# The second block's down projection as seven block products, with weight sums made by accumulating DMAs

## The reference

```python
h = _rmsnorm(x, g_ffn)
x = x + (jax.nn.silu(h @ w1) * (h @ w3)) @ w2        # w2: 2816 x 1024
gate = jax.nn.sigmoid(_rmsnorm(x, g_ple) @ w_ple_gate)
x = x + gate * (p_i @ w_ple)
return _rmsnorm(x, g_final)
```

## Time and profile before

| | us |
|---|---|
| median of three runs | 2056.28 (2055.24 to 2057.49) |
| span of the profiled execution (first to last instruction) | 2052.9 |
| what lies around the span, against the median | 3.4 |
| TensorE busy | 1952.2 |
| granted TensorE clock, mean | 0.979 |

### The profile page before, as it was taken

The page is one execution under the profiler, slowest core; times in us unless marked ns, Lnnn a source line. Parts: engine busy times, 40 slices in busy tenths (PEclk is TensorE's granted clock), DMA queues, the critical chain, the costliest instruction groups (busy, mean ns, idle before and its releaser), DMA issues.

```text
span 2052.9 us, 22852 instructions
## 1 busy us (share of the span) xinstructions
PE 1952.2 (95%) x9422; PEld 1211.6 (59%) x9422; DVE 730.4 (36%) x1069; ACT 532.1 (26%) x828; POOL 118.6 (6%) x127
## 2 busy tenths in 40 slices
PE   8999999989899897989899899999999999999998
PEld 6867843333333332323333368878888888888886
DVE  5648331101001010100101067595588443345225
ACT  5236220101000000101000056334444332234125
POOL 3432000000000000000000000141000000000000
PEclk9999999999999999999999999999999999999999
DMA  9420789999999999999999933212114222323331
GB/s 273 144 72 18 297 342 430 427 431 429 431 430 432 432 430 427 432 430 429 431 434 425 423 128 134 82 43 83 62 62 146 101 83 82 119 85 113 109 140 59
DMA packets 42295, 517.33 MB, mean 252 GB/s; under 512 B 5216, under 2 KB 5344, under 8 KB 12656
## 3 DMA queue, kind: packets, MB, share of 16 engines
q1 hardware_dynamic: 39728, 508.39, 60.6%
q0 software_dynamic: 2496, 7.92, 1.8%
HBM read 508.92 MB, written 6.29 MB: 251 GB/s over the span
## 4 chain that ended last, share of the span: by engine, by line
PE 73%; DMA 20%; DVE 5%; ACT 1%; issue 1%; POOL 0%; SPq 0%; ACTq 0%; DVEq 0%
DMA arena<-in_w_gu_dram 19%; PE bank L2517 15%; PE bank L2542 6%; PE bank L964 4%; PE bank L963 4%; PE bank L962 4%; PE bank L601 3%; PE bank L602 3%; PE bank L603 3%; PE bank L2479 2%; PE bank L994 2%; PE bank L993 2%; PE bank L995 2%; PE bank L2143 2%; PE bank L2149 2%; PE bank L2145 2%
## 5 line engine op out<-in xcount | busy, mean ns | idle before, releaser
L2517 PE MATMUL bank<-arena 128*64 128x512 f32 x2048 | 480.3, 625 | 67.8 <-DMA arena<-in_w_gu_dram 63.9
L2517 PEld LDWEIGHTS bank<-arena 128*64 128x64 f32 x2048 | 163.1, 143 | 360.2 <-issue 348.0
L3014 DVE TENSOR_TENSOR arena<-arena,bank 128x256 f32<-128x256 f32 x64 | 27.0, 421 | 639.6 <-ACT arena L3255 639.6
L2542 PE MATMUL bank<-arena 128*64 128x512 f32 x1024 | 232.6, 595 | 0.6 <-ACT arena L3259 0.6
L3255 ACT ACTIVATE arena<-bank 128x256 f32<-128x256 f32 x64 | 24.6, 384 | 537.0 <-PE bank L2517 537.0
L2542 PEld LDWEIGHTS bank<-arena 128*64 128x64 f32 x1024 | 73.7, 137 | 139.2 <-issue 139.2
L962 PE MATMUL bank<-input_rounded,weight_rest 128*128 128x512 f32 x352 | 137.2, 390 | 0.0
L964 PE MATMUL bank<-input_rounded,weight_rounded 128*128 128x512 f32 x352 | 137.0, 389 | 0.0
L963 PE MATMUL bank<-input_rest,weight_rounded 128*128 128x512 f32 x352 | 137.0, 389 | 0.0
L601 PE MATMUL bank<-input_rounded,weight_rest 128*128 128x512 f32 x312 | 125.9, 403 | 1.2 <-DVE weight_rest L1050 1.2
L603 PE MATMUL bank<-input_rounded,unit_rounded 128*128 128x512 f32 x312 | 122.4, 392 | 0.0
(11 more groups left out here) (528 smaller groups left out, 2851.1 us busy)
## 6 DMA issues: line engine op xcount, KB each, us to landing
arena<-in_w_gu_dram SPq DMA_DIRECT2D x47, 4096.0 KB, 28.9
arena<-in_w_d_dram SPq DMA_DIRECT2D x62, 2048.0 KB, 26.5
arena<-in_wpack_dram SPq DMA_DIRECT2D x83, 1024.0 KB, 5.0
arena<-in_w_gu_dram SPq DMA_DIRECT2D x32, 2048.0 KB, 17.4
arena<-in_w_d_dram SPq DMA_DIRECT2D x4, 1024.0 KB, 10.0
arena<-in_w_gu_dram SPq DMA_DIRECT2D x3, 1024.0 KB, 8.3
arena<-in_xT_dram SPq DMA_DIRECT2D x4, 512.0 KB, 7.2
arena<-in_x_dram SPq DMA_DIRECT2D x2, 1024.0 KB, 13.2
```

The costliest lines, as they stand in the source:

```text
L2517: last = mm(ab[64 * x:64 * x + 64, :], xsT[:, k, 64 * x:64 * x + 64], w[x][k], start=k == 0, stop=k == KD - 1)
L2542: last = mm(bank[4 + n][64 * x:64 * x + 64, :], hidT[c % 2][:, P * t + 64 * x:P * t + 64 * x + 64], w[:, x, t, 512 * n:512 * n + 512], sta ...
```

## The change

The hidden activations A (512 tokens by 2816) are cut into four blocks: the first and last 256 tokens by the first and last 11 hidden tiles, A11, A12 (first tokens), A21, A22. The weights `w2` are cut alike into B0 (first 11 tiles, first 512 columns), B1 (first tiles, last columns), B2 (last tiles, first columns), B3. Seven products of 11 hidden tiles, two token tiles and 512 columns take the place of eight:

- p1 = A11·B0, ue = (A21−A22)·(B0+B1), p2 = A12·B2, wb = (A11+A21−A22−A12)·B3, vg = (A11+A21−A22)·(B0+B1+B3), zf = (A11+A21)·(B1+B3), hh = A22·(B0+B1+B2+B3).

They run in this order, each in three chunks d of 4, 4 and 3 hidden tiles, so 7 x 11 x 2 x 3 = 462 matmuls. The sums of A are made on VectorE during the up stage (`token_sums`: one addition of 128x256 a tile for the first 11, three for the others). The results reach `x_res` by 22 additions of 128x512 (`down_sums`) in place of eight. The rounded part of a product's activations lies where an operand of an earlier product was.

The sums of weights are made by transfers that add to what lies there (`accum_op=ALU.add`), issued by GpSimd: `grown[d]` is loaded with B0 by SyncE at the end of the up stage and then has B1, B3 and B2 added, each for the next of ue, vg, hh; the chunks of zf are loaded with B1 into the ring and have B3 added there. That is 12 adding transfers of 1 MB or 0.75 MB. Chunks of p1, p2 and wb come by the ring as before.

VectorE's and ScalarE's loops over the up stage are written out. The last gates take the units of the first 256 tokens first, and turning these tokens stands behind zf's second chunk. `hn`, `pw`, `fsilu` and the gate's inputs lie elsewhere.

```diff
+DOWN = ("p1", "ue", "p2", "wb", "vg", "zf", "hh")
+DOWN_GROWN = ("ue", "vg", "hh")
+ADDED = ("ue", "vg", "zf", "hh")
+DOWN_WEIGHT = {"p1": 0, "p2": 2, "wb": 3, "zf": 1}
+DOWN_KS = (range(0, 4), range(4, 8), range(8, HT))
+N_DOWN = 3 * len(DOWN)
...
-GATE_ORDER = [(0, 0), (1, 0), (2, 0), (3, 0), (0, 1), (1, 1), (2, 1), (3, 1)]
+GATE_ORDER = [(0, 0), (1, 0), (0, 1), (1, 1), (2, 0), (3, 0), (2, 1), (3, 1)]
...
+        part_at = {name: B + BLK * i for i, name in enumerate(("a11", "a12", "u", "w", "v", "z", "a22"))}
+        raw_part = {name: view(at, BLK) for name, at in part_at.items()}
+        part_of = {"p1": "a11", "ue": "u", "p2": "a12", "wb": "w", "vg": "v", "zf": "z", "hh": "a22"}
+        part_lo = {m: [rounded(f"down_rest_{m}_{d}", part_at[name] + TOK * ks[0], TOK * len(ks)) for d, ks in enumerate(DOWN_KS)]
+                   for m, name in part_of.items()}
+        hi_at = {"ue": T0 + 1280, "p2": part_at["a11"], "wb": part_at["u"], "vg": part_at["a12"], "zf": part_at["w"],
+                 "hh": part_at["v"]}
+        part_hi = {m: [rounded(f"down_rounded_{m}_{d}", at + TOK * ks[0], TOK * len(ks)) for d, ks in enumerate(DOWN_KS)]
+                   for m, at in hi_at.items()}
...
+        down_bank = {"p1": (4, 5), "ue": (6, 7), "p2": (2, 3), "wb": (4, 5), "vg": (0, 1), "zf": (2, 3), "hh": (0, 1)}
...
+            def add_weights(to, block, d):
+                pool.dma_start(to, A["wpack"][C_DOWN + 3 * block + d][:, 0:512 * len(DOWN_KS[d])], accum_op=ALU.add)\
+                    .then_inc(S(f"added_in{d}"), 16)
+
+            for d in range(3):
+                pool.wait_ge(S(f"grown_in{d}"), nth(f"grown_in{d}", 16))
+                add_weights(grown[d], 1, d)
+            for d in range(3):
+                pool.wait_ge(S(f"added_in{d}"), nth(f"added_in{d}", 16))
+                pool.wait_ge(S("wlo_made"), NFT + 3 * DOWN.index("ue") + d + 1)
+                add_weights(grown[d], 3, d)
+            for d in range(3):
+                c = C_DOWN + 3 * DOWN.index("zf") + d
+                pool.wait_ge(S(f"added_in{d}"), nth(f"added_in{d}", 32))
+                pool.wait_ge(S(f"chunk_in{c % R}"), LANDED[c])
+                add_weights(down_raw(c), 3, d)
+            for d in range(3):
+                pool.wait_ge(S(f"added_in{d}"), nth(f"added_in{d}", 48))
+                pool.wait_ge(S("wlo_made"), NFT + 3 * DOWN.index("vg") + d + 1)
+                add_weights(grown[d], 2, d)
...
+            for m, name in enumerate(DOWN):
+                for d, ks in enumerate(DOWN_KS):
+                    c = C_DOWN + 3 * m + d
+                    if d == 0:
...
+                    pe.wait_ge(S("alo_made"), rests_upto(m, d))
+                    pe.wait_ge(S("wlo_made"), NFT + 3 * m + d + 1)
                     wh = whi[c % R].rearrange("p (k n) -> p k n", n=512)
                     wl = wlo[c % R].rearrange("p (k n) -> p k n", n=512)
-                    for i in range(NT):
+                    for i in range(2):
+                        b = bank[down_bank[name][i]][:, :]
                         for k in ks:
...
+                            mm(b, down_lo(name, k, i), wh[:, k - 4 * d, :], start=k == 0, stop=False)
+                            mm(b, down_hi(name, k, i), wl[:, k - 4 * d, :], start=False, stop=False)
+                            last = mm(b, down_hi(name, k, i), wh[:, k - 4 * d, :], start=False, stop=k == HT - 1)
+                    last.then_inc(S("down_chunk"), 1)
+                    if name == "zf" and d == 1:
+                        pe.wait_ge(S("down_added"), nth("down_added", 14))
+                        turn_tokens(0, range(KD))
+                    if name == "hh" and d == 1:
+                        pe.wait_ge(S("down_added"), nth("down_added", 18))
+                        pe.wait_ge(S("norm_tv"), 3 * KD)
+                        turn_tokens(1, range(4, KD))
 
```

VectorE's sums of the activations, and SyncE's loads:

```diff
+            def token_sums(f):
+                k = f % HT
+                dve.wait_ge(S("act_made"), f + 3)
+                a11, u = tile_part("a11", k), tile_part("u", k)
+                if f < HT:
+                    own(tt(out=tile_part("z", k), in0=a11, in1=u, op=ALU.add))
+                    return
+                if k == 0:
+                    own.wait()
+                own(tt(out=u, in0=u, in1=tile_part("a22", k), op=ALU.subtract))
+                own.wait()
+                own(tt(out=tile_part("v", k), in0=u, in1=a11, op=ALU.add))
+                own.wait()
+                tt(out=tile_part("w", k), in0=tile_part("v", k), in1=tile_part("a12", k), op=ALU.subtract)\
+                    .then_inc(S("sums_made"), 1)
...
+            def part_rest(m, d):
+                name = DOWN[m]
+                dve.wait_ge(S("ahi_made"), rests_upto(m, d))
+                a = slice(TOK * DOWN_KS[d][0], TOK * (DOWN_KS[d][-1] + 1))
+                tt(out=part_lo[name][d], in0=raw_part[part_of[name]][:, a], in1=part_hi[name][d], op=ALU.subtract)\
+                    .then_inc(S("alo_made"), 1)
+
+            def down_rest(m, d):
+                c = C_DOWN + 3 * m + d
+                n = 512 * len(DOWN_KS[d])
+                dve.wait_ge(S("whi_made"), NFT + 3 * m + d + 1)
+                tt(out=wlo[c % R][:, 0:n], in0=down_raw(c), in1=whi[c % R][:, 0:n], op=ALU.subtract).then_inc(S("wlo_made"), 1)
...
+            for m in range(1, len(DOWN)):
+                if m >= 2:
+                    down_sums(m - 2)
+                for d in range(3):
+                    part_rest(m, d)
+                    down_rest(m, d)
+                    if DOWN[m] == "hh" and d == 0:
+                        for k in range(KD):
+                            gate_lo(dve, 0, k)
+                        half_scales(dve, 0)
```

```diff
+                if not in_ring(c):
+                    name, d = down_at(c)
+                    if name == DOWN_GROWN[0]:
+                        if d == 0:
+                            sp.wait_ge(S("up_filled"), 2 * NFT)
+                        elif d == 2:
+                            sp.wait_ge(S("down_chunk"), 2)
+                        sp.dma_start(grown[d], wpack[C_DOWN + d][:, 0:512 * len(DOWN_KS[d])]).then_inc(S(f"grown_in{d}"), 16)
+                    continue
...
+                if C_DOWN <= c < C_PG:
+                    sp.dma_start(down_raw(c), wpack[from_dram(c)][:, 0:512 * len(DOWN_KS[down_at(c)[1]])])\
+                        .then_inc(S(f"chunk_in{c % R}"), 16)
...
+                if c == C_PG:
+                    sp.wait_ge(S("down_chunk"), 18)
                     sp.dma_start(pw.rearrange("p i d -> p (i d)"), ple_kept).then_inc(S("ple_back"), 16)
+            sp.wait_ge(S("wlo_made"), NFT + N_DOWN)
+            sp.dma_start(grow, A["gfin"].partition_broadcast(P)).then_inc(S("gfin_in"), 16)
             tiles = out.rearrange("a (i p) d -> i p (a d)", p=P)
```

More of the change, by code:

```diff
@@ L68, with down_at, in_ring, from_dram @@
 N_CHUNKS = C_PG + N_PG
-C_FIRST = N_CHUNKS
-C_PLE = N_CHUNKS + 1
+D_PG = C_DOWN + 12
+D_FIRST = D_PG + N_PG
+D_PLE = D_FIRST + 1
+def down_at(c):
+    m, d = divmod(c - C_DOWN, 3)
+    return DOWN[m], d
+def in_ring(c):
+    return not C_DOWN <= c < C_PG or down_at(c)[0] not in DOWN_GROWN
+def from_dram(c):
+    if c < C_DOWN:
+        return c
+    if c >= C_PG:
+        return D_PG + c - C_PG
+    name, d = down_at(c)
+    return C_DOWN + 3 * DOWN_WEIGHT[name] + d
+LANDED = {}
+_count = [0] * R
+for _c in range(N_CHUNKS):
+    if in_ring(_c):
+        _count[_c % R] += 16
+    LANDED[_c] = _count[_c % R]
 NSLOT = 8
@@ L501, in program @@
         bhi = [rounded(f"branch_rounded{i}", B + 14336 + WCH * i, WCH) for i in range(2)]
-        actT = view(B + 4096, NFT, L)
-        alo = [rounded(f"hidden_rest{k}", B + 4096 + 512 * k, L) for k in range(NFT)]
-        pw = view(B + 4096, NT, D)
+        pw = view(B + 4608, NT, D)
         pgate = [view(B + 16384 + 512 * i, 512) for i in range(4)]
@@ new lines, in second_dve @@
+            for f in range(NFT):
+                if f % 2 == 0 and f < NFT - 2:
+                    weight_rests(C_UP + f + 2, f + 3)
+                if f == 18:
+                    first_rest(0)
+                if f == 20:
+                    down_rest(0, 0)
+                    first_rest(1)
+                    first_rest(2)
+                act_tile(f)
+                token_sums(f)
+            first_rest(3)
+            down_rest(0, 1)
+            first_rest(4)
+            down_rest(0, 2)
```

395 lines of the change are left out of this document (243 added, 152 removed).

## The result

The changed kernel takes **2071.78 us** (median of 4 runs, 2067.71 to 2072.27); the kernel before 2055.76 (4 runs, 2053.60 to 2057.49). The ratio is 1.007, 95% interval 1.0058 to 1.0083: slower by 16 us by the medians and by 14 by the ratio, where 5.5 us less were forecast and 2064 was the upper end of the range. The profiled execution took 2071.57 us with a span of 2069.8.

What follows compares the result with a forecast made beforehand. TensorE's matmuls, one behind the other, were taken as the bound. −15.0 + 0.3 + 5.0 + 3.6 + 0.6 = −5.5 us, from 2056.3 to 2050.8 us; range 2041.5 to 2064.

Steps and rivals of the forecast that it cites:

- What bounds the kernel, the gain of 15.0: Down stage: TensorE's matmuls are the path, so 66 fewer at 0.2267 us each save 15.0 us.
- p1's second chunk, 0.3: Start of the down stage: VectorE's weight rest for this chunk comes late, so TensorE waits 0.3 us.
- The weights of ue: Deciding term, ahead of ue's first chunk: 3.3 us late plus 1.7 for the lost clock, 5.0 us.
- X − 4.1: TensorE's wait ahead of ue's first chunk, given an adding transfer of X us; forecast at 3.3 us.
- X: Time of GpSimd's adding 1 MB transfer, issue to landing: taken as 7.4 us, bounds 5.0 and 16.4.
- My test for the step: GpSimd's 1 MB transfers land in about 7.4 us; below 6 or above 9, the main step is wrong.
- my own sign: The frame is wrong if TensorE waits at p2, wb or vg, or the up stage's 247 us grow.
- The weights of the others: Products after ue: vg's additions 35 us ahead, zf 3.6 us with clock, hh's second chunk and the gates 0.6.
- X − 5.5: TensorE's wait ahead of zf's first chunk, given an adding transfer of X us; forecast at 1.9 us.
- Slow additions: Rival at ue and zf: adding transfers eat up the gain at X = 10.2; 2066 at X = 15; chance 0.19.
- As quick as plain loads: Rival: additions take X = 5.0 to 5.5, ue waits little, zf not at all; 2043.4 us, chance 0.25.
- VectorE becomes the bound: Rival: six products each start with a 1 us wait while VectorE catches up; 2057, chance 0.14 including other handovers.

Runs made afterwards that it cites:

- e2_none: Changed kernel without GpSimd's twelve down-stage transfers, sums of weights left out: 2043.2 us.
- e1_plain: Changed kernel with the twelve adding transfers as plain loads of the same bytes, sums of weights left out: 17 to 18 us faster than the changed kernel.
- e5_hold: Changed kernel with vg's additions held until wb's last chunk has landed: 3.3 us faster by the ratios.
- e4_gates: Changed kernel with the gate inputs of the first 256 tokens made behind hh's second chunk instead of its first: same ratio as the changed kernel.
- e8_turns: Kernel with order p1, p2, wb, ue, vg, zf, hh and zf's chunks in own memory, now one adding transfer at a time: some 22 us above the expected 2055.
- e12_vg_hold: Reordered kernel with zf's chunks in own memory, ue's additions held for wb's second chunk, now vg's additions issued ahead of zf's: 2049.3 us.
- e11_ue_adds: Changed kernel in which only ue's three transfers add, the other nine fetching plainly: no time in the text; ue waits 4.99 us.
- e3_order: Changed kernel with products in the order p1, p2, ue, wb, vg, zf, hh, all sums made: 2058.3 us.
- e7_spread: Changed kernel with order p1, p2, wb, ue, vg, zf, hh, and zf's chunks loaded 30 to 45 us ahead into own memory: 2054.5 us.

## Why the prediction was wrong

**What bounds the kernel, the gain of 15.0.** Right: e2_none shows 13.9 of it over stage and gates.

**p1's second chunk, 0.3.** Right; it doesn't show above 0.3.

**The weights of ue, the step that decides.** "X − 4.1" was nearly right and X alone was well bounded. ScalarE's and GpSimd's timelines:

```profile
1888.63 0.90 POOL L716 DMA_DIRECT2D arena<-in_wpack_dram  x1 [464.47 <-DMA arena<-in_wpack_dram]
1891.11 0.85 POOL L716 DMA_DIRECT2D arena<-in_wpack_dram  x1 [1.58 <-DMA arena<-in_wpack_dram]
...
1904.89 1.72 POOL L716 DMA_DIRECT2D arena<-in_wpack_dram  x2 [12.93 <-DMA arena<-in_wpack_dram]
```

```profile
1896.55 1.91 ACT L2030 ACTIVATE weight_rounded<-arena 128x2048 fp32r<-128x2048 f32 x1 [8.18 <-DMA arena<-in_wpack_dram]
...
1904.51 1.92 ACT L2030 ACTIVATE weight_rounded<-arena 128x2048 fp32r<-128x2048 f32 x1 [5.11 <-DMA arena<-in_wpack_dram]
```

The first addition took 7.9 us from issue to ScalarE's start, where my X was 7.4; without adding (e1_plain) the same transfer landed in 5.7. By the halved rate that the Trainium skill states (Collectives: The Full Stack, "The bandwidth ceiling: the fold count and why AG ≠ RS ≠ AR") my estimate had been 7.9, and the trace agrees with it. That it is the second fetch which costs the time, and not something else of the same size, no run here separates. `grown[0]` itself landed 1.5 us later than I had it (8.3 behind the stage's start, not 6.8), as three loads left together. 7.9 − 4.1 + 1.5 = 5.3, measured 5.07. With the clock ue cost about 7, not 5.0.

But the second addition, issued 2.5 us behind the first, took 13.4. **The step that failed is that X is one number**, 7.4 us wherever an addition stands, and that additions cost nobody else anything. The sentence "the second and third additions run behind the first ... and don't come late" took each transfer as if it had the DMA engines to itself. At ue itself that did little harm: TensorE waited 0.21 and 0.55 us ahead of these two chunks. It is at zf, wb and hh that the sharing costs. Here only additions are under way (zf's third and hh's first two), to be held against 426 GB/s at a share of 0.99 in the earlier trace rows:

```profile
1979.00:1982.00 3.00, 3.00 (x15) 2.49 (x14) 2.13 (x2) 0.11 (x1) 0.00 (x0) 1.00 1.03 205
```

All engines full at 205 GB/s: a megabyte (1.05 million bytes) holds them for 5.1 us, where a plain one holds them for 2.5. Twelve transfers of 11 MB together are some 56 us of full engines. My test for the step was a landing outside 6 to 9 us: it was 12.7. By my own sign the frame was wrong too, since TensorE waits at wb.

**The weights of the others.** "vg's additions start some 35 us ahead" was read as harmless. They were, for vg; they ran from 1904.89 beside p2's and wb's plain loads, and wb waited 2.36 (e5_hold). I had asked when each transfer would be ready, and never whom it would delay. The engines then stood idle for 15 us:

```profile
1936.00:1951.00 15.00, 13.27 (x59) 11.03 (x60) 15.00 (x11) 11.84 (x10) 0.00 (x0) 1.00 0.02 6
```

zf: "X − 5.5", with the right X of its place, is right again. GpSimd issues at 1958.55, ScalarE starts at 1969.71: 11.2, and 5.7 is near the 6.19 measured. The forecast of 1.9 was mis-sized by X alone. hh: its three additions leave beside zf's and beside each other, so that the first lands late and pushes the gate inputs back, and these the rounding of the second chunk (see e4_gates); 3.94 where I had 0.3.

By terms, with the clock lost behind each wait: ue 7.3 us where I had 5.0, zf 7.6 where I had 3.6, hh's second chunk 5.7 where I had 0.3, wb 2.4 and the turning of the tokens ahead of the gates 1.0 where I had nothing.

**The rivals.** "Slow additions" had the mechanism and the sign, with 0.19. It put 2066 at X = 15, and the kernel landed at 2071.8 with X = 7.9 for the first addition and 12.7 on the median; its break-even of X = 10.2 was passed. What it lacked are the plain loads that additions slow, at wb. Its last sentence, in which the three additions of a product are longer under way than TensorE works on one, came nearest to what the runs show. "As quick as plain loads" fails by e1_plain; that the value I gave it, 2043.4, is the time of e2_none, in which they aren't there, is chance. "VectorE becomes the bound" is out by e2_none.

**Not explained.** 2.6 us of the stage and the gates, the 0.8 behind them, and the 3.4 us ahead of the stage. That the chip would give back e2_none's last 6 us by a still better order wasn't tried.

## What to carry to other kernels

Price a transfer twice: by its latency alone, and by how long it holds the DMA engines, summed over all that run at that time; a latency taken in a quiet stretch says nothing about three at once. An adding transfer counts about double in that sum (5.1 us against 2.5 for a megabyte here), and it takes the time from plain loads that somebody needs sooner, so give the needed loads the engines first, start additions into the gaps, and let the order in the issuing engine's list be the order in which the results are needed. A hold that frees one product moves the queue: follow the list behind the held instruction to its end, with the semaphores that its transfers share.

## What the runs showed of the hardware

Accumulating transfers of 1 MB from memory into SBUF by GpSimd: 7.7 to 7.9 us with next to nothing beside them (e8_turns), 10.9 and 13.0 beside plain loads (e8_turns), 11.6 to 14.2 as medians where several are under way; 205 GB/s with the engines full, against 426 for plain loads.

The clock did not follow the length of the wait, as my 1.7 us "for every wait of 2 us or more" had it. In e1_plain TensorE waits 2.84 us ahead of ue:

```profile
1898.88 0.47 PE L1150 MATMUL bank<-weight_rounded,down_rest_ue 128*128 128x512 f32 x1 [2.84 <-DVE weight_rest L1632]
```

and keeps its clock:

```profile
1898.00:1901.00 3.00, 2.12 (x9) 1.80 (x10) 1.87 (x2) 1.68 (x1) 0.55 (x2) 1.00 0.80 314
```

In e12_vg_hold a wait of 1.80 us ahead of vg, from 1943.3, loses it:

```profile
1945.10 0.47 PE L1158 MATMUL bank<-weight_rounded,down_rest_vg 128*128 128x512 f32 x1 [1.80 <-DVE weight_rest L1640]
```

```profile
1947.00:1949.00 2.00, 2.00 (x6) 1.55 (x5) 1.45 (x1) 1.25 (x2) 0.00 (x0) 0.50 1.00 205
```

0.50 is the lower of the two levels, 1.2 GHz. In the changed kernel the clock fell in or behind each of the waits of 5.07, 6.19 and 3.94 us (5.4 us lost in all), behind that of 2.36 it did not. The longest wait that kept it is hh's in e5_hold:

```profile
1997.39 0.47 PE L1153 MATMUL bank<-weight_rounded,down_rest_hh 128*128 128x512 f32 x1 [3.42 <-DVE weight_rest L1635]
```

```profile
1999.00:2002.00 3.00, 3.00 (x15) 2.47 (x14) 3.00 (x5) 0.00 (x0) 0.00 (x0) 1.00 0.49 197
```

Against it, 2.06 us in e11_ue_adds, 2.11 in e3_order and 3.11 in e7_spread lost it. For waits of 1.8 to 3.4 us a loss of the clock is a chance, not a term; all of 3.9 us and more lost it here.
